# Moving element-wise work between engines and stages of a two-block transformer kernel: modulation products, context squares, and the residual adds of the norm between the blocks

## The reference, cut to what matters

```python
silu_c, silu_cc = silu(c)[:, None, :], silu(c_ctx)
for l in range(DEPTH):
    mx = split(silu_c @ w_mod[l] + b_mod[l], 6)    # for the 512 rows
    mc = split(silu_cc @ w_mod[l] + b_mod[l], 6)   # for the 256 context rows
    ax = modulate(rmsnorm(h, norm1_g[l]), mx[0], mx[1])
    ac = modulate(rmsnorm(hc, norm1_g[l]), mc[0], mc[1])
    ... = mixing_layer(ax @ w_in[l], ac @ w_in[l], ...)
```

## Time and profile before

| | us |
|---|---|
| median of 3 runs | 2882.94 (2882.17 to 2884.89) |
| the profiled execution | 2882.23, of which the span is 2880.5 |
| PE busy | 2790.3 (97%) |
| DVE busy | 1777.1 (62%) |
| ACT busy | 1145.6 (40%) |
| POOL busy | 161.7 (6%) |
| mean granted TensorE clock | 0.993 of full |

### The profile page before, as it was taken

The page is one execution under the profiler, slowest core; times in us unless marked ns, Lnnn a source line. Parts: engine busy times, 40 slices in busy tenths (PEclk is TensorE's granted clock), DMA queues, the critical chain, the costliest instruction groups (busy, mean ns, idle before and its releaser), DMA issues. The chain is left out here.

```text
span 2880.5 us, 35972 instructions
## 1 busy us (share of the span) xinstructions
PE 2790.3 (97%) x14607; PEld 2369.5 (82%) x14607; DVE 1777.1 (62%) x2729; ACT 1145.6 (40%) x1762; POOL 161.7 (6%) x179
## 2 busy tenths in 40 slices
PE   9999999999899999989989999999999999999998
PEld 8657888888477888779965999999998975788887
DVE  6677867678768767467766565435534137674563
ACT  5254524443535334332255343213323236553342
POOL 0101000010110000100020100000000002100001
PEclk9999999999999999999999999999999999999999
DMA  5303243243122343216620111121112131232322
GB/s 208 110 16 124 91 143 118 88 140 117 44 96 88 99 140 98 76 64 216 226 85 34 59 66 59 58 74 59 64 56 71 60 103 41 89 103 85 111 86 84
DMA packets 85205, 269.96 MB, mean 94 GB/s; under 512 B 9264, under 2 KB 14256, under 8 KB 84656
## 3 DMA queue, kind: packets, MB, share of 16 engines
q1 hardware_dynamic: 85040, 267.66, 28.0%
HBM read 265.52 MB, written 2.10 MB: 93 GB/s over the span
## 5 line engine op out<-in xcount | busy, mean ns | idle before, releaser
L1396 PE MATMUL PS<-HH,WH 128*128 128x512 f32 (+2 forms) x3148 | 1038.0, 361 | 27.1 <-DVE HL L874 11.5
L1396 PE MATMUL PS<-HH,WL 128*128 128x512 f32 (+2 forms) x3148 | 1026.8, 358 | 0.0
L1396 PE MATMUL PS<-HL,WH 128*128 128x512 f32 (+2 forms) x3148 | 1026.7, 358 | 0.0
L1192 DVE TENSOR_TENSOR WL<-STAGE,WH 128x1024 fp32r<-128x1024 f32 (+2 forms) x420 | 478.1, 1140 | 475.8 <-ACT WH L1186 475.2
L1396 PEld LDWEIGHTS PS<-HH,WH 128*128 128x128 f32 x3148 | 584.8, 189 | 104.6 <-DVE HL L874 14.3
L1186 ACT ACTIVATE WH<-STAGE 128x1024 fp32r<-128x1024 f32 (+2 forms) x420 | 407.5, 972 | 614.7 <-DMA STAGE<-in_w_down 263.1
L1396 PEld LDWEIGHTS PS<-HL,WH 128*128 128x128 f32 x3148 | 585.0, 189 | 64.8 <-issue 2.4
L1396 PEld LDWEIGHTS PS<-HH,WL 128*128 128x128 f32 x3148 | 585.0, 189 | 62.8
L1396 PE MATMUL PS<-GH,WH 128*128 128x512 f32 (+2 forms) x913 | 305.0, 363 | 0.0
L1396 PE MATMUL PS<-GH,WL 128*128 128x512 f32 (+2 forms) x913 | 302.8, 361 | 0.0
L1396 PE MATMUL PS<-GL,WH 128*128 128x512 f32 (+2 forms) x913 | 302.8, 361 | 0.0
(11 more groups left out here) (241 smaller groups left out, 2433.9 us busy)
## 6 DMA issues: line engine op xcount, KB each, us to landing
STAGE<-in_w_up SPq DMA_DIRECT2D x176, 512.0 KB, 3.2
MODBUF<-in_w_mod SPq DMA_DIRECT2D x96, 512.0 KB, 4.2
STAGE<-in_w_in SPq DMA_DIRECT2D x84, 512.0 KB, 3.4
STAGE<-in_w_down SPq DMA_DIRECT2D x64, 384.0 KB, 3.1
STAGE<-in_w_down SPq DMA_DIRECT2D x64, 320.0 KB, 2.9
STAGE<-in_w_out SPq DMA_DIRECT2D x32, 512.0 KB, 4.5
BM<-in_na_bias SPq DMA_DIRECT2D x24, 256.0 KB, 2.5
CR<-in_const_ret SPq DMA_DIRECT2D x2, 1152.0 KB, 5.2
```

Of the source, the lines that this page charges most:

```text
L1192: dve.tensor_tensor(WL[unit.slot][:, 0:size], STAGE[unit.slot][:, 0:size], WH[unit.slot][:, 0:size].bitcast(F32), ALU.subtract).then_inc(w ...
L1396: ins = pe.matmul(self.acc(tile, col, tn, p), w[:, c:c + P], r[:, k, t0:t0 + tn], start=(k == 0 and m == 0 and not (joined and p)), stop=( ...
```

## The change

The products of `out1` are hung one on each of tiles 0 to 5 instead of two on tiles 1 to 4, and the two that this leaves over are hung on tiles 11 and 17 of the first up projection. `CtxPrep` is split: `CtxSums` (squares and adds) hangs on the first down projection, `CtxNorm` (mean, HH, HL) on tiles 1 to 4 of the second. In the crossing all 16 residual adds go to GpSimd; VectorE scales up to three chunks ahead and makes its early `WL` after the first half's scaling; PE sums the squares of the second half two chunks ahead, and runs the third tile three chunks behind the first two; ScalarE makes the first half's RSTD before the second half's first squares.

```diff
-    def pool(self, pool, prep=None):
+    def pool(self, pool):
...
-            if prep:
-                prep.pool(pool, c)
...
+    BEHIND = 3
...
+        act.wait_ge(xsq_summed.sem, xsq_summed.at(self.x0 + DC))
+        self.norm.act(act)
...
-        act.wait_ge(xsq_summed.sem, xsq_summed.at(self.x0 + DC))
-        self.norm.act(act)
...
-        def summed(i):
-            p, c = divmod(i, DC)
-            rows = self.rows(p)
-            dve.wait_ge(y_scaled.sem, y_scaled.at(self.y0 + i + 1))
-            dve.tensor_tensor(X[:, c, rows], X[:, c, rows], Y[:, c, rows], ALU.add).then_inc(added.sem, 1)
...
-        scaled(0)
...
-            if c + 1 < DC:
-                scaled(c + 1)
-            summed(c)
-            if c == 1:
+            scaled(c)
+            if c == 2:
...
-            if c == 5:
-                for u in self.early:
-                    self.run.split_low(dve, u)
+        for u in self.early:
+            self.run.split_low(dve, u)
...
-        scaled(DC)
-        scaled(DC + 1)
-        summed(DC)
-        summed(DC + 1)
+        for c in range(3):
+            scaled(DC + c)
...
-            if c + 2 < DC:
-                scaled(DC + c + 2)
-                summed(DC + c + 2)
+            if c + 3 < DC:
+                scaled(DC + c + 3)
...
+    def pool(self, pool):
+        for i in range(2 * DC):
+            p, c = divmod(i, DC)
+            rows = self.rows(p)
+            pool.wait_ge(y_scaled.sem, y_scaled.at(self.y0 + i + 1))
+            pool.tensor_tensor(X[:, c, rows], X[:, c, rows], Y[:, c, rows], ALU.add).then_inc(added.sem, 1)
...
-        for p in range(2):
-            for c in range(DC):
-                self.wait_lo(pe, DC + DC * p + c)
-                for tile in first:
-                    self.run.pe_chunk(pe, tile, c, 0, halves_of(SEQ)[p], final=p == 1)
-                if p == 0:
-                    squares_summed(DC + c)
-class CtxPrep:
-    def __init__(self, head):
-        self.head = head
-        self.counts = dict(csq_done=DC, csq_added=DC - 1, csq_summed=1)
+        def x(p, k, tiles):
+            self.wait_lo(pe, DC + DC * p + k)
+            for tile in tiles:
+                self.run.pe_chunk(pe, tile, k, 0, halves_of(SEQ)[p], final=p == 1)
+        for c in range(2):
+            squares_summed(DC + c)
+        for k in range(DC):
+            x(0, k, first[0:2])
+            if k + 2 < DC:
+                squares_summed(DC + k + 2)
+            if k >= self.BEHIND:
+                x(0, k - self.BEHIND, first[2:])
+        for k in range(DC - self.BEHIND, DC):
+            x(0, k, first[2:])
+        for k in range(DC):
+            x(1, k, first)
+class CtxSums:
+    counts = dict(csq_done=DC, csq_added=DC - 1)
     def act(self, act, run, tile):
-        t, head = tile.t, self.head
-        if t == 0:
+        if tile.t == 0:
...
-        if t < 4:
-            for c in (2 * t, 2 * t + 1):
+        if tile.t < 4:
+            for c in (2 * tile.t, 2 * tile.t + 1):
...
-        if t == 4:
+    def pool(self, pool):
+        for c in range(1, DC):
+            pool.wait_ge(csq_done.sem, csq_done.at(c + 1))
+            if c > 1:
+                pool.wait_ge(csq_added.sem, csq_added.at(c - 1))
+            first = SQ[0] if c == 1 else SQSUM
+            pool.tensor_tensor(SQSUM[:, SEQ:TOK], first[:, SEQ:TOK], SQ[c % 2][:, SEQ:TOK],
+                               ALU.add).then_inc(csq_added.sem, 1)
+    def dve(self, dve, run, tile):
+        pass
+    def pe(self, pe, run, tile):
+        pass
+class CtxNorm:
+    counts = dict(csq_summed=1)
+    def __init__(self, head):
+        self.head = head
+    def act(self, act, run, tile):
+        if tile.t == 0:
...
-            head.ctx_norm.act(act)
-        for c in self.chunks(t):
-            head.high(act, c)
+            self.head.ctx_norm.act(act)
+        for c in self.chunks(tile.t):
+            self.head.high(act, c)
     def chunks(self, t):
-        return range(3 * t - 12, min(3 * t - 9, DC)) if 4 <= t < 7 else ()
+        return range(2 * t - 2, 2 * t) if 1 <= t < 5 else ()
...
-        if tile.t == 4:
+        if tile.t == 1:
...
-            if c > chunks[0]:
-                self.head.low(dve, c - 1)
-        for c in chunks[-1:]:
+        for c in chunks:
...
-    def pool(self, pool, t):
-        if t <= 4:
-            for c in (2 * t - 2, 2 * t - 1):
-                if c == 0:
-                    continue
-                pool.wait_ge(csq_done.sem, csq_done.at(c + 1))
-                if c > 1:
-                    pool.wait_ge(csq_added.sem, csq_added.at(c - 1))
-                first = SQ[0] if c == 1 else SQSUM
-                pool.tensor_tensor(SQSUM[:, SEQ:TOK], first[:, SEQ:TOK], SQ[c % 2][:, SEQ:TOK],
-                                   ALU.add).then_inc(csq_added.sem, 1)
     def pe(self, pe, run, tile):
-        if tile.t == 5:
+        if tile.t == 1:
...
+            pe.wait_ge(mod_done.sem, mod_done.at(2 * MOD_N))
...
-                    seg.sums.pool(pool, seg.prep)
+                    seg.sums.pool(pool)
+                if isinstance(seg.prep, CtxSums):
+                    seg.prep.pool(pool)
...
-                    mods=lambda t: 2 if 1 <= t < 5 else 0, halved=1)]
-def ffn1(l, prep=None):
+                    mods=lambda t: 1 if t < 6 else 0, halved=1)]
+def ffn1(l, preps=(None, None)):
...
-                    tap_col=V1_FCW, late=True, together=1 if half else 4 - l),
+                    tap_col=V1_FCW, late=True, together=1 if half else 4 - l,
+                    mods=lambda t, half=half: 1 if half == 0 and t in (11, 17) else 0),
...
-                    prep=prep if half else None, halved=half)]
+                    prep=preps[half], halved=half)]
...
-run = Run([(MixHead(VEC1[1], HH1, HL1), out1(1)), (post(1), ffn1(1, CtxPrep(crossing))), (crossing, in2(0))], 4,
+run = Run([(MixHead(VEC1[1], HH1, HL1), out1(1)), (post(1), ffn1(1, (CtxSums(), CtxNorm(crossing)))), (crossing, in2(0))], 4,
```

## The result

The changed kernel takes 2854.98 us, the median of 4 runs (2853.52 to 2855.92), where the kernel before took 2883.01 (2882.17 to 2884.89, 4 runs): ratio 0.9901, 95% interval 0.9884 to 0.9919, 28.0 us less. The forecast was 2851.2 with a range of 2844 to 2861. The profiled execution took 2853.52, of which 2851.8 are the span, against 2880.5: 28.7 us less.

A forecast was written before the change was run, and what follows sets the result against it. PE, busy 97% of the span, was taken as the bound, so only its waits and the clock after them could give time. 6.95 + 4.3 + 7.7 + 12.7 = 31.7 us off 2882.2, plus 0.7, gave 2851.2, range 2844 to 2861.

The forecast's parts named there:

- Part 1, layer 0: Layer 0 output projection: one product per tile shortens VectorE's loop, saving 4.3 us of wait plus 2.65 of clock, 6.95 us.
- Layer 1: Layer 1 output projection: same spreading, but a later start leaves PE a 2.2 us wait; 4.3 us saved.
- the guess of half of 2.65: Layer 1 output projection: clock after the 2.2 us wait left open, so half of the 2.65 us was counted.
- The two products in the up projection: Products on up projection tiles 11 and 17 fit where VectorE idles 2.17 us per pair of tiles; cost nothing.
- Part 2, the context: Context's mean in the last down projection: PE's 5.70 us wait and 2.0 us of clock go, 7.7 us saved.
- Part 3, the crossing: Crossing: PE's sums two chunks ahead open a ring of waits; 14.2 us instead of 26.9, saving 12.7 us.
- All three terms of the 14.2 us (12.0 + 1.3 + 0.9): Crossing: PE's pure work 12.0 us, its waits 1.3, and its later arrival from the first half's longer chain 0.9.
- The adds holding the crossing (1): Crossing: GpSimd's adds taking turns with VectorE keep PE waiting in most chunks; 8 us saved there, 2856; chance 0.14.
- The output projections staying late (2): Both output projections: waits remain and the clock still falls; 3 + 1.5 saved instead of 11.3, 2858; chance 0.11.
- Rival 3: Whole kernel better than worked out: turns hidden, no clock lost in layer 1, 2846; chance 0.09.
- 4: Crossing: each SBUF port hand-over costs microseconds in the 16 adds, making the kernel slower, about 2890; chance 0.02.
- 5: Whole kernel: no effect, since PE's waits only end a chain another resource sets (weights by DMA); chance 0.02.

The follow-up runs named there:

- E12: Changed kernel with crossing adds back on VectorE, 14 idle PE matmuls before block two's first up projection, one more product moved to the up projection; 2852.44 us.
- E8: Changed kernel with no products on the output projections, all eight on odd tiles 5 to 19 of the first up projection; 2853.73 us.
- E9: Changed kernel with all eight products on up projection tiles 3 to 17 (odd), and the condition's copy and context's load moved; 2862.28 us.
- E5: Changed kernel with the crossing's 16 residual adds back on VectorE; 2852.95 us.
- E6: Changed kernel with PE's old order of sums and chunks in the crossing, adds still on GpSimd; 2864.96 us.
- E10: E9 plus 14 idle PE matmuls in the 2.71 us wait ahead of block two's first up projection; 2859.6 us.

## Why the prediction was right, point by point

**Part 1, layer 0** (forecast 6.95, measured 6.72): right. The loop is 3.97 us (forecast 3.98), the wait 0.39 (0.3), and no slow window follows. But the reason given for the loop, VectorE's time less one product, is only half of it. That the second product goes takes 1.14 us off; what is left is the ring through ScalarE, 3.72 us long. Whoever had gone on with the working's rule (1.14 us per product) would have been wrong, as E12's expectation was.

**Layer 1** (4.3, measured 3.70): right in kind. The wait is 2.33 instead of 2.2, which gives 2.8 us where 2.95 were put. The rest of the miss is the clock. From the sum's first matmul to the mark it takes 4.54 us at full clock (layer 0), 7.04 in layer 1 before and 6.12 after, so 0.9 us of clock came back, where the guess of half of 2.65 had 1.3. In all eight traces with a wait of 2.15 to 2.54 us there, this stretch takes 6.03 to 6.13 us. What makes layer 1 later than layer 0 is mostly ScalarE's copy of the condition, which takes 1.90 us where the waits differ by 1.94. But ScalarE also waits for the weights behind the context's load, as the forecast had it:

```profile
836.47 1.06 ACT L1199 ACTIVATE WH<-STAGE 128x1024 fp32r<-128x1024 f32 x1 [0.85 <-DMA STAGE<-in_w_out]
```

With the products out and the copy and load left in (E8) the wait is 1.14 us, with all three out (E9) it is nothing. The copy and the load were not moved singly.

**The two products in the up projection** (0, measured 0): right. No wait of PE on `WL` or `GL` there. The cover named was the right one and has a limit: eight products in these tiles cost 3.9 us in layer 0 and nothing in layer 1 (E8). A likely reason, argued and not tested by itself, is that the idle time in the steady part of a stage is what the engine needs to catch up with what was late at its beginning.

**Part 2, the context** (7.7, measured 7.82, alone 7.8): right. The mean runs without a wait, and neither the first nor the second down projection has a new one.

**Part 3, the crossing** (12.7, measured 13.38): right in its mechanism, 0.7 too low. All three terms of the 14.2 us (12.0 + 1.3 + 0.9) were off, and their errors partly cancel. PE waits only 0.26 us on `HL` in that loop, where 1.3 were put, and comes 0.4 us later, where 0.9 were put; but its own work, from its sums of chunks 0 and 1 (1236.21) to its first matmul of the second half (1249.25), less that wait, takes 12.8 us, where 12.0 were put. Together 13.4 instead of 14.2. VectorE's chunk takes 1.67 us, forecast 1.8, and GpSimd's add with its turn 0.98, forecast 1.0. That PE hardly waits although VectorE's chunk is longer than its own work fits the third tile, run three chunks behind, which gives it other work; no run takes that tile back alone. The rows show the turns: `T` is recorded with 0.84 instead of 0.48 us beside an add, an instruction with an input from PSUM with its usual 0.41. The page "SBUF — State Buffer" of the Trainium skill, section "Who interferes with whom", states that a VectorE instruction with two SBUF inputs contends with a GpSimd instruction that reads SBUF, and one with at most one SBUF input, outside its two-port modes, does not. These rows agree with it. The forecast's conclusion that the adds themselves gain nothing is right to 0.64 us (E5), and that the gain is the reordering's is shown by E6.

**The sum.** 31.7 forecast, 31.6 in the four stretches. That they agree to 0.1 us is luck: the crossing gave 0.7 more, and the two output projections 0.2 and 0.6 less. The total came out 3.8 us above the forecast all the same. In the profiled execution 3.0 of it are the 2.75 us of the rest with 0.2 of the two other stretches, for which there was no term; the median lies 1.5 us above that execution, where 0.7 was added. The text held that after a wait of 2.7 us the clock stayed at 1.00, and took this one row for a property of the place. It was one outcome of two. That the drop comes from the idle time is supported by E10 to E12 (none in three traces), with seven of eleven without. That is not proof: if each trace had the chance of 4 in 11 to go without a drop, three in a row would do so about one time in twenty. Why it falls in one execution and not in another is open.

**The rivals.** The adds holding the crossing (1) would have needed waits of PE in most chunks: there is one of 0.26 us. The output projections staying late (2) holds for layer 1 in part, which still waits 2.33 us and loses clock; the two gave 10.4 us, where this rival had 4.5. Rival 3 had it right that the turns are nearly hidden, but layer 1 did lose clock, and the time is far from its 2846. Both of the last (4, 5) are out.

## What to carry to other kernels

Where PE waits the same time in every turn of a loop, look for a ring of buffers that closes through PE itself: PE's new order, with the sum two steps ahead and one tile behind, is worth 13.8 us here (E6), the adds on an idle engine 0.6 (E5). Before moving a second and third piece of work off an engine, work out the next ring of the loop, because the first removal may already have made it the bound. Idle time in the middle of a stage may be no free room if the engine enters that stage late, and a load that is moved in a queue takes its own wait along to everything behind it.

## What the runs showed of the hardware

The same wait of PE, 2.70 to 2.71 us long, with the same work ahead of it and behind it, was followed by a granted clock of 1.00 in four traces, of 0.50 to 0.75 in seven, at a price of about 1.5 to 2.8 us. Behind the shorter wait at the end of layer 1's output projection, 2.15 to 2.54 us, all eight traces lost about 1.5 us of clock, and behind one of 1.14 us at the same place (E8) none was lost. So with waits of this length the trace of one execution doesn't tell what the next will do: differences of 3 us between kernels can be this and nothing else, and only stretches between marks tell a change of 1 us. With fourteen idle matmuls in the wait there was no drop in any of three traces, and the real work came about 0.2 us later.
